# A mixture-of-experts decoder step: TensorE's expert loop written out, ScalarE's and VectorE's folded to one body, and the order of a block changed

## What is computed

```python
logits = h @ w_router + b_router
top_v, top_i = lax.top_k(logits, 4)
gates = softmax(top_v)
...
def expert_block(args):              # xb: the rows of one block, e: its expert
    xb, e = args
    a = jnp.dot(xb, w1[e]) + b1[e]
    x_glu = jnp.minimum(a[:, :D_FF], 7.0)
    x_lin = jnp.clip(a[:, D_FF:], -7.0, 7.0)
    mid = x_glu * jax.nn.sigmoid(1.702 * x_glu) * (x_lin + 1.0)
    return jnp.dot(mid, w2[e]) + b2[e]
...
out = sum over the token's experts of gate * block row;  x = x + out
```

## Time and profile before

| | before |
|---|---|
| time, median of 3 | 1232.85 us (1230.18 to 1238.05) |
| the profiled execution's span | 1236.6 us |
| PE busy | 1085.0 us, 88% |
| DVE busy | 411.4 us, 33% |
| ACT busy | 219.6 us, 18% |
| HBM read | 442.46 MB |
| mean over the span | 360 GB/s |

### The profile page before, as it was taken

One profiled execution on the slowest core, in us unless ns is written; L12 is line 12 of the kernel. 1 busy time (PEld: TensorE's weight loads), 2 busy tenths in 40 slices (PEclk: granted clock), 3 DMA queues, 4 the chain that ended last, 5 costly groups with the idle time before them and its releaser, 6 DMA issues.

```text
span 1236.6 us, 29830 instructions
## 1 busy us (share of the span) xinstructions
PE 1085.0 (88%) x10851; PEld 496.2 (40%) x10852; DVE 411.4 (33%) x1237; ACT 219.6 (18%) x402; POOL 79.2 (6%) x117
## 2 busy tenths in 40 slices
PE   5998789989989798999999776899989968997996
PEld 4775445544334243344433332244334413443442
DVE  4899746452222222222222221122222212221222
ACT  3213434121111110111111010011111100110112
POOL 2159500000000000000000000000000000000000
PEclk9998989999989999999999898799999998997999
DMA  8426592973999999999999999999999999999995
GB/s 247 169 86 210 192 356 103 366 307 160 420 419 419 421 414 419 420 420 387 418 420 419 420 418 420 421 378 420 419 419 382 419 421 421 401 420 420 419 419 215
DMA packets 81007, 446.41 MB, mean 361 GB/s; under 512 B 16769, under 2 KB 18113, under 8 KB 32001
## 3 DMA queue, kind: packets, MB, share of 16 engines
q1 hardware_dynamic: 80896, 445.00, 89.3%
HBM read 442.46 MB, written 2.51 MB: 360 GB/s over the span
## 4 chain that ended last, share of the span: by engine, by line
PE 60%; DMA 15%; SPq 13%; issue 6%; DVE 3%; ACT 1%; DVEq 1%; POOL 0%; POOLq 0%; ACTq 0%
PE ps L1721 21%; SPq L483 11%; PE ps L1729 10%; PE ps L1666 4%; DMA ring<-in_w_moe_dram 4%; PE ps L1316 4%; PE ps L1698 3%; PE ps L1714 3%; DMA w_glu<-in_w_moe_dram 2%; PE ps L1586 2%; DMA low<-in_w_moe_dram 2%; DMA uni<-in_w_moe_dram 2%; DMA kv_rows<-in_w_moe_dram 2%; DMA ring<-in_cache_k_dram 2%; PE ps L1709 1%
## 5 line engine op out<-in xcount | busy, mean ns | idle before, releaser
L1721 PE MATMUL ps<-ring,uni 128*32 128x512 f32 x2008 | 244.6, 624 | 46.3 <-issue 31.2
L1721 PEld LDWEIGHTS ps<-ring,uni 128*32 128x32 f32 x2008 | 63.8, 113 | 220.8 <-issue 186.4
L1224 DVE TENSOR_SCALAR uni<-ps 128x256 f32<-128x256 f32 x51 | 21.6, 424 | 294.2 <-PE ps L1721 294.2
L1729 PE MATMUL ps<-ring,uni 128*32 128x256 f32 x1696 | 100.3, 381 | 7.5 <-DMA ring<-in_w_moe_dram 7.5
L792 ACT ACTIVATE uni<-uni 128x256 f32<-128x256 f32 x51 | 21.2, 416 | 423.4 <-DVE uni L1224 423.4
L1245 DVE COPY uni<-ps 128x256 f32<-128x256 f32 x50 | 21.2, 425 | 216.5 <-PE ps L1709 216.5
L1666 PE MATMUL ps<-uni 128*32 128x256 f32 x1248 | 80.4, 392 | 8.7 <-DVE uni L1239 8.3
L792 ACT ACT_TABLE_LOAD x51 | 65.4, 1283 | 85.2 <-issue 85.2
L1729 PEld LDWEIGHTS ps<-ring,uni 128*32 128x32 f32 x1696 | 51.9, 110 | 46.5 <-DMA ring<-in_w_moe_dram 11.7
L1316 PE MATMUL ps<-accT,ring 128*128 128x288 f32 x256 | 65.7, 416 | 0.0
L1698 PE MATMUL ps<-uni 32*128 32x256 f32 x832 | 62.0, 413 | 0.0
(11 more groups left out here) (388 smaller groups left out, 1262.2 us busy)
## 6 DMA issues: line engine op xcount, KB each, us to landing
ring<-in_w_moe_dram SPq DMA_DIRECT2D x222, 1024.0 KB, 24.1
tmp<-in_w_moe_dram SPq DMA_DIRECT2D x36, 1024.0 KB, 24.5
kv_rows<-in_w_moe_dram SPq DMA_DIRECT2D x18, 1024.0 KB, 23.6
w_glu<-in_w_moe_dram SPq DMA_DIRECT2D x18, 1024.0 KB, 26.4
mixer<-in_w_moe_dram SPq DMA_DIRECT2D x18, 1024.0 KB, 25.3
uni<-in_w_moe_dram SPq DMA_DIRECT2D x18, 1024.0 KB, 26.2
accT<-in_w_moe_dram SPq DMA_DIRECT2D x18, 1024.0 KB, 26.2
x<-in_w_moe_dram SPq DMA_DIRECT2D x18, 1024.0 KB, 26.6
```

The source lines that it names most:

```text
L1721: ins = mm(hidden(q), xe[:, k % 2, quarter(k // 2)], slot(turn, k)[:, :, NQ * q:NQ * q + NQ], start=False, stop=(k == 7), skip_group_check ...
L1729: ins = mm(ps[quarter(q), 7, 0:NQ], mt[:, m, quarter(k - 8)], slot(turn, k)[:, m, NQ * q:NQ * q + NQ], start=(k == 8 and m == 0), stop=(k ...
```

## The change

- TensorE's loop over experts is written out: all 32 experts stand one behind the other, with fixed wait values. ScalarE and VectorE have one body for one expert in a loop of 32. SP's stream is not touched.
- `second_biases` comes after the sixteenth expert and not after the twenty-eighth.
- In a block, TensorE does `sum_back(2)` ahead of the gather, the transposes of `selg` ahead of those of `mid`, and `gathered_columns` and `first_bias` of the next block ahead of the second products.
- VectorE copies `mt` after `xs` and not ahead of `pick`.

```diff
--- before.py
+++ after.py
@@ -58,6 +58,7 @@
 NPIECE = 12
 NSLOT = 21
 TURNS = 7
+BIAS_TURN = 15
 
 
 C_ID, C_GM, C_TRI, C_BP, C_BS, C_IOTA, C_QM = 0, 128, 256, 384, 768, 1600, 1984
@@ -332,7 +333,7 @@
             done = eng.alloc_register()
             eng.reg_mov(done, 0)
 
-            def expert(turn, e, before):
+            def expert(turn, e):
                 count = eng.value_load(cnt[0:1, bass.ds(e, 1)], min_val=1, max_val=NTOK)
                 name = expert_at(eng, e) if named else None
                 with eng.Fori(0, 2 * CAP, CAP) as p:
@@ -343,16 +344,17 @@
                                     with eng.If(count > c):
                                         n = eng.snap(done, min_val=0, max_val=NEXP * CHUNKS)
                                         first = nc.s_assert_within(c, 0, CHUNKS * CAP - CAP, skip_runtime_bounds_check_because="p, o, c of the three loops give 0; 1, 2; 3 to 8 times CAP")
-                                        block_of(n, turn, name, before, first)
+                                        block_of(n, turn, name, first)
                                         eng.reg_add(done, done, 1)
 
-            with nc.Fori(0, NEXP // TURNS, engines=[eng.engine], hint_back_edge=eng is nc.tensor) as g:
-                for turn in range(TURNS):
-                    expert(turn, g * TURNS + turn, g * (16 * TURNS * NPIECE // NSLOT))
-            if between:
-                between()
-            for turn in range(NEXP % TURNS):
-                expert(turn, NEXP // TURNS * TURNS + turn, 16 * (NEXP // TURNS * TURNS * NPIECE // NSLOT))
+            if eng is nc.tensor:
+                for turn in range(NEXP):
+                    expert(turn, turn)
+                    if turn == BIAS_TURN:
+                        between()
+            else:
+                with nc.Fori(0, NEXP, engines=[eng.engine]) as e:
+                    expert(None, e)
             return eng.snap(done, min_val=NEXP, max_val=NEXP * CHUNKS)
 
 
...
@@ -1229,6 +1231,8 @@
                 dve.wait_ge(S["swc"], n * 2 + 1)
                 dve.wait_ge(S["sgm"], n)
                 tt(mid, lin, sig, ALU.mult).then_inc(S["midr"], 1)
+
+            def mid_columns(n):
                 dve.wait_ge(S["mt_ps"], n)
                 dve.tensor_copy(mt, ps[:, 7, 0:NQ].rearrange("p (m c) -> p m c", c=P)).then_inc(S["mt"], 1)
 
@@ -1241,12 +1245,13 @@
                 dve.tensor_copy(pick, bc(stack[:, bass.ds(e, 1)], [P, CAP])).then_inc(S["pick"], 1)
                 dve.wait_ge(S["gath"], n + 1)
                 dve.tensor_copy(xs, ps[:, 6, 0:NQ]).then_inc(S["xs"], 1)
+                mid_columns(n)
                 dve.wait_ge(S["xeT_ps"], n + 1)
                 dve.tensor_copy(xe, ps[:, 6, NQ:2 * NQ].rearrange("p (m c) -> p m c", c=P)).then_inc(S["xe"], 1)
                 dve.wait_ge(S["sel"], n + 1)
                 gated_selection(bc(gate[:, bass.ds(e, 1), :].rearrange("p e t -> p (e t)").unsqueeze(2), [P, 3, CAP]))
 
-            def dve_pass(n, turn, e, before, first):
+            def dve_pass(n, turn, e, first):
 
                 with dve.If(n > 0):
                     next_block(n, e, first)
@@ -1257,6 +1262,7 @@
             gating(total)
             dve.memset(st[:, 91:92], 0.0).then_inc(S["pick"], 1)
             dve.memset(st[:, 92:93], 0.0).then_inc(S["xs"], 1)
+            mid_columns(total)
             dve.wait_ge(S["ss"], 3)
             ts(st[:, 63:65], st[:, 60:62], 1.0 / D, EPS, ALU.mult, ALU.add)
             dve.wait_ge(S["ssq"], 2)
@@ -1713,17 +1719,17 @@
                 for q in range(4):
                     mm(hidden(q), pick[quarter(q), :], b1_rows[quarter(q), :].rearrange("p (g n) -> p g n", g=2), start=True, stop=False, skip_group_check=True)
 
-            def pe_pass(n, turn, e, before, first):
+            def pe_pass(n, turn, e, first):
 
                 def first_product(k):
-                    pe.wait_ge(landed(turn, k), before + loads(turn, k))
+                    pe.wait_ge(landed(turn, k), loads(turn, k))
                     for q in range(4):
                         ins = mm(hidden(q), xe[:, k % 2, quarter(k // 2)], slot(turn, k)[:, :, NQ * q:NQ * q + NQ], start=False, stop=(k == 7),
                                  skip_group_check=True)
                     return ins
 
                 def second_product(k):
-                    pe.wait_ge(landed(turn, k), before + loads(turn, k))
+                    pe.wait_ge(landed(turn, k), loads(turn, k))
                     for m in range(2):
                         for q in range(4):
                             ins = mm(ps[quarter(q), 7, 0:NQ], mt[:, m, quarter(k - 8)], slot(turn, k)[:, m, NQ * q:NQ * q + NQ],
@@ -1738,18 +1744,21 @@
                     else:
                         ins.then_inc(S["w_used"], 1)
                 pe.wait_ge(S["y"], n + 1)
+                pe.wait_ge(S["selT"], n + 1)
                 sum_back(0)
                 sum_back(1).then_inc(S["w_used"], 1)
+                sum_back(2)
                 gather(n + 1)
                 pe.wait_ge(S["midr"], n + 1)
-                for m in range(2):
-                    ins = tp(ps[:, 7, P * m:P * m + P], mid[:, m::2], ident)
-                ins.then_inc(S["mt_ps"], 1)
-                sum_back(2)
                 pe.wait_ge(S["selg"], n + 2)
                 for t in range(3):
                     ins = tp(ps[:, 5, P * t:P * t + P], selg[:, t, :, :].rearrange("p q s -> p (q s)"), ident)
                 ins.then_inc(S["selT_ps"], 1)
+                for m in range(2):
+                    ins = tp(ps[:, 7, P * m:P * m + P], mid[:, m::2], ident)
+                ins.then_inc(S["mt_ps"], 1)
+                gathered_columns(n + 1)
+                first_bias()
                 pe.wait_ge(S["mt"], n + 1)
                 for k in range(8, NPIECE):
                     ins = second_product(k)
@@ -1757,8 +1766,6 @@
                         ins.then_inc(S["out_ps"], 1)
                     else:
                         ins.then_inc(S["w_used"], 1)
-                gathered_columns(n + 1)
-                first_bias()
 
             gathered_columns(0)
             pe.wait_ge(S["cntr"], 1)
```

More of the change, by code:

```diff
@@ L789, in _, with act_pass @@
             A(gT[2 * NEXP:, 0:NS], ps[2 * NEXP:3 * NEXP, 7, SEQ:SEQ + NS], ACT.Copy).then_inc(S["gT"], 1)
-            def act_pass(n, turn, e, before, first):
+            def act_pass(n, turn, e, first):
                 act.wait_ge(S["glin"], n + 1)
```

## The result

The changed kernel takes 1256.92 us (median of 4 runs, 1254.74 to 1258.51), the kernel before 1234.47 us beside it. The ratio is 1.019, with a 95% interval of 1.016 to 1.022. It is slower, by 1.6 to 2.2%; 1226 us was forecast, and the range ended at 1242 us. The profiled execution's span is 1252.6 us against 1236.6 us.

The account below looks back on a forecast made before the run. TensorE sets the end with the weight stream 3.5 us behind; after the change the stream decides. +0.6 - 4.3 - 3.0 = -6.7 us on 1236.6 gives 1229.9 us, less 3.75 us to the median: 1226 us, range 1214 to 1242.

Parts of the forecast that it names:

- The way into the next expert: TensorE's idle between one expert's last block and the next expert: 1.6 us taken in place of 1.15 us, ends 1.15 and 2.06.
- The third rival: Way into an expert grows to 2 us and the clock falls: +8 us over the present, 1241 us; chance 0.15.
- TensorE's new wait: In each block, `gathered_columns` waits for ScalarE's copy of the three transposes: 0.3 us a block, ends 0 and 0.66 us.
- The first slot: Two blocks lie ahead of the first slot's return, so the weight stream starts 0.6 us later: +0.6 us.
- The stream: Weight stream gets shorter through earlier slot returns and no VectorE restarts: -4.3 us, ends 0 and the whole 13.2 us.
- the -3.6 us: Three-block experts return their first slot 0.8 us sooner at five dips in the weight stream, the first giving only 0.4 us.
- The -0.7 us: VectorE's loop restarts and their code fetches go: a quarter of the 2.8 us of stream shortfall outside the dips.
- The second biases: Moved from near the end to mid-way: free while TensorE waits there for data, about 3 us without that cover.
- The -12.3 us: TensorE's time after 1037 us: the second biases' 13.9 us there replaced by a plain way in of 1.6 us.
- The tail: From the last weight landing to the first `sum_back` of the kernel's end: 1.6 us in place of 5.0, taken as -3.0 us.
- VectorE and ScalarE: Both mostly idle; VectorE's restart at every expert is as short a jump as 0.92 us, so their term is 0.
- a rival with 0.04: VectorE's and ScalarE's jump misses at every expert, each restart costing 1.5 us of weight stream: 1270 us; chance 0.04.

Follow-up runs that it names:

- the first experiment: The changed kernel with the order of work inside a block put back as before on TensorE and VectorE, all else changed: 1229.63 us, ratio 0.9972.

## Why the prediction was wrong, step by step

**The way into the next expert: the step that failed.** The prediction saw the mechanism: about 0.9 us hides under `first_bias`, and less will hide behind second products. It then took 1.6 us, "half way". Behind a one-block expert it was 2.08 to 2.19 us, above even its upper end of 2.06 us; that any of it hid does not show. The upper end was read from ScalarE's bookkeeping, which is not TensorE's. The clock behind it was taken as full, and was low in 22 of 31 ways in. Three things made the price of that wrong.
- The step spoke only of ways into another expert. A way into the next block of the same expert also has branches, 0.75 us behind the first block; it showed no idle before only because it was covered. Thirteen such places were at zero in the sum, about 10 us together.
- The cover was counted as `first_bias` alone. The two transposes of `gathered_columns` cover as well. Idle in front of a next expert by what stands last in the block: nothing 2.1 us; four products (1.06 us) 1.6 us; two products (1.05 us) 1.3 us; transposes and four products (1.49 us) 1.2 us (1.3 in looped code). Read the other way, from the end of the second products to the next expert's first it takes 2.1 us with nothing between, 2.3 with two products, 2.6 with four and 2.6 with transposes and four: 1.0 to 1.4 us of work there lengthens the way by 0.2 to 0.5 us.
- The clock was left at full in the forecast, since 1.6 us lay below the 1.99 us of its one row with a low clock. At 2.1 us 15 of the 18 ways in behind a one-block expert start at the low clock. And the kernel before already had it in all seven ways in behind a two-block expert (idle 2.0 to 2.9 us), which the prediction used only for the price of a rival. Against the first experiment's kernel, which has the same instructions in another order, TensorE's busy time from the first block to the last grew by 16.0 us (832.7 to 848.7), the clock's price on balance.

**The third rival was the truth, and too cheap.** It named the mechanism, a longer idle and a low clock behind it, with a chance of 0.15, and put the point from which it decides at about 2.0 us of idle. For the one-block experts that came true; as a rule it does not hold (see the last section). Its price of +8 us counted six ways in near the end and 1 to 2 us at five dips. But there is no slack under the stream to hide in once TensorE is behind everywhere. From the first block's first products to the last block's it is 962.0 us against 946.0. TensorE's idle in front of first products grew by 33 us (82.1 us at entries and between blocks, 49.2 us before, both summed over all blocks), the new wait adds 19.5 us, and its busy time grew by 8.6 us. In that last term are 15 x 1.7 = 25 us more of low clock at the entries, less what the products that waited for data had lost to the low clock before. Taken back were 31.2 us of waits for data (42.6 to 11.4), 8.3 us of waiting for VectorE's `sel`, and 5.3 us of idle at the second biases: +61 - 45 = +16 us. From about 300 us on TensorE and not the stream set the pace in most blocks. The prediction counted TensorE's terms only after 1037 us and let the stream decide; with the way in at 1.6 us and a full clock that seemed enough.

**TensorE's new wait.** 0.39 us a block against 0.3, within its ends. Same-expert blocks take 16.19 us against 16.1. Right in size. That it hides under the stream is right only nearly: with the cover in place (`first_bias` last) the kernel was 2.1 us slower than the one in the old order beside it, and its stream took 922.7 us against 919.5.

**The first slot.** +0.6 was taken. From the first block's first product to the first weight behind the blank it is 35.6 us against 33.8 us, +1.8. The two blocks' new waits (2 x 0.39) are as forecast; the 0.75 us in front of the second block, and what else the longer blocks add, were not in it.

**The stream: the right number for the wrong reason.** -4.3 us was forecast, of which -3.6 from the block's new order and -0.7 from VectorE's restarts. With the old order and the rest of the change it is -4.4 us, and with one looped body alone -4.7 us. So the whole gain is the restarts', and that the total agreed is luck. The order gives none: with `first_bias` last, which leaves only the order and the wait, the stream is 3.2 us longer than in the old order. The premise of the -3.6 us, that in the dips the first block's second products wait for data, was not so in the block at 536.85 us, ahead of the dip to 373 GB/s. In the whole new order the dips did not get shallower; two became standstills of 7 us, because the ways in ahead of a three-block expert now push its slots back by more than the 0.8 us that was to be won. The -0.7 us was worked out from 2.8 us of shortfall outside the dips, but 2.4 us of these are the last of the 40 slices, where the weights run out (168 GB/s from 1218 to 1220 us, 37 GB/s behind). What the restarts cost lies mostly in the dips: up to 1211 us these lose 9.7 to 9.9 us against 420 GB/s in the three kernels with groups of seven, about 7 us in the four with one body and the old order. With the restarts went both the gather's waits for `sel` (8.3 us) and half of one queue's packets of instructions (40 to 19 between 300 and 1211 us). Which of the two the stream gained from stays open.

**The second biases.** Near the end or mid-way made no difference that could be measured, in two pairs of runs. The -12.3 us on TensorE's side were right as a reading (4.6 us mid-way in place of 13.9 us), but no path ran through them.

**The tail.** -3.0 us did not come: the last weight moved until 1231.3 us, and TensorE's second products ran to 1240.1 us, at their own pace. With the old order it waits for the last pieces, and 13.1 us remain from the last weight to the end against 15.9 before. That is -2.8 us, close to the forecast, but without the change that the term was built on.

**VectorE and ScalarE.** At 0, right. VectorE's longest idle is 5.5 us rather than 3 to 4, the gather waits for nobody. The rule of the Trainium skill ("Runtime: NRT & Kernel Launch", Instruction fetch mechanics), that kernels prefer full unrolling because a taken branch out of the small window stalls, was weighed there as a rival with 0.04. The runs split it. On VectorE the smallest loop beat the group of seven (0.9979 by itself, with an interval that touches 1, and 4.7 us of stream). On TensorE writing out gave nothing that could be measured in the old order and 20 us in the new one.

## What to carry to other kernels

Branches and register work at the end of a block are free only as long as the engine still has work queued when its sequencer reaches them; what stands last in the loop body is that cover. Here a few long instructions covered part of the way and 64 short passes (3.59 us) did not keep it under 2.1 us, so try the few long ones last. When costing a reorder, sum the idle over every block boundary that shows none today, and ask of each whether it is short or merely covered. A wait or a few tenths of a microsecond inside a block may be free where a stream sets the pace, while an idle time that lowers the clock is paid twice.

## What the runs showed of the hardware that was not expected

- The length of idle does not settle the clock by itself. In the changed kernel 2.1 to 2.2 us of idle behind a one-block expert was followed by the low clock in 15 of 18 cases; two of the other three waited for data inside their first products, and one had the full clock. Behind a three-block expert, with 2.13 to 2.17 us, it was followed by it in 1 of 6. Behind a two-block expert the kernel before had it in seven of seven (idle 2.0 to 2.9 us), the first experiment's, with 2.0 to 2.2 us, in three of seven. With two products last, 2.1 to 2.2 us was followed by it in 4 of 7; behind less than 1.8 us and no wait for data no profile shows it.
- The cover that long products give is not their duration. 1.05 us in four matrix passes hid 0.8 us of branches, 1.06 us in eight passes hid 0.55 us. That fits a sequencer that needs its own time for each instruction ahead of the branches, but it was not tried apart.
- Four 32-row products on four quarters of the array take together what two of them take, 1.05 us.
- TensorE's jump back over seven written-out experts costs 2 to 3 us of idle in the old order, and 6.8 to 9.9 us at five of six places in the new order (3.8 at the sixth), with or without the cover. The body is as long in both, with the same hint in the code. A late VectorE does not tell them apart: with one body on VectorE, where the gather never waits for it, the jumps in the old order take 2 to 3 us as well. What makes the jump miss stays open.
